# A pooling mixer fed from a transposed copy of the input, with its neighbour sums on VectorE

## The reference, cut to what matters

```python
h = rms_norm(x, g_mix)
for g, win in enumerate((2, 4, 8, 16)):          # 256 channels each
    mean = (cs[t + win//2] - cs[t - win//2]) / cnt    # centred window, cut at the sequence's ends
    d[g] = mean - h[:, slice(g)]
y = einsum('bsgc,gce->bsge', d, pool_w) * pool_scale
x = x + y
a = relu(rms_norm(x, g_mlp) @ w_up)
x = x + (a * a) @ w_down
return rms_norm(x, g_fin)
```

## Time and profile before

| | |
|---|---|
| median of 3 runs | 1790.71 us (1789.93 to 1791.59) |
| the profiled execution | 1790.22 us, its span 1788.4 |
| busy, share of the span | PE 98%, PEld 82%, DVE 63%, ACT 43%, POOL 9% |
| granted TensorE clock, mean | 0.996 |
| DMA | 432.67 MB, 242 GB/s |

### The profile page before, as it was taken

One profiled execution on the slowest core, in us unless ns is written; L12 is line 12 of the kernel. 1 busy time (PEld: TensorE's weight loads), 2 busy tenths in 40 slices (PEclk: granted clock), 3 DMA queues, 4 the chain that ended last, 5 costly groups with the idle time before them and its releaser, 6 DMA issues.

```text
span 1788.4 us, 20968 instructions
## 1 busy us (share of the span) xinstructions
PE 1756.3 (98%) x8156; PEld 1461.8 (82%) x8156; DVE 1122.7 (63%) x1178; ACT 761.4 (43%) x1186; POOL 158.7 (9%) x139
## 2 busy tenths in 40 slices
PE   8999999999999999999999999999999999999996
PEld 8888887778888888888888888888888888888885
DVE  6678888786555564765555647645556575445447
ACT  6556554554343335344333344343333543233232
POOL 4000112001001120010011200000112010000001
PEclk9999999999999999999999999999999999999998
DMA  7597766668856665668666555776665657666654
GB/s 266 218 348 281 265 252 242 245 263 326 307 212 224 223 224 212 247 242 295 243 223 223 213 212 204 280 295 223 224 224 212 235 205 273 240 223 239 233 202 163
DMA packets 80902, 432.67 MB, mean 242 GB/s; under 512 B 8860, under 2 KB 10780, under 8 KB 42916
## 3 DMA queue, kind: packets, MB, share of 16 engines
q1 hardware_dynamic: 57764, 347.44, 52.6%
q10 hardware_dynamic: 23040, 83.90, 13.8%
HBM read 360.00 MB, written 71.30 MB: 241 GB/s over the span
## 4 chain that ended last, share of the span: by engine, by line
PE 89%; DVE 6%; ACT 1%; DMA 1%; issue 1%; POOL 1%; ACTq 0%; SPq 0%; POOLq 0%; DVEq 0%
PE up_ps L1169 16%; PE up_ps L1171 16%; PE up_ps L1170 16%; PE ring_ps L1188 13%; PE ring_ps L1190 13%; PE ring_ps L1189 13%; DVE m_acc L832 1%; PE ring_ps L1213 1%; DVE w_slot L765 1%; PE ring_ps L1215 1%; PE ring_ps L1214 1%; DVE a_slot L773 1%; PE mix_ps L1198 1%; DVE wu_lo L756 1%; DMA wd_raw<-w_down 1%
## 5 line engine op out<-in xcount | busy, mean ns | idle before, releaser
L756 DVE TENSOR_TENSOR wu_lo<-wu_raw,wu_hi 128x1024 fp32r<-128x1024 f32 x158 | 195.8, 1239 | 579.7 <-ACT wu_hi L496 579.7
L1169 PE MATMUL up_ps<-h_hi,wu_hi 128*128 128x512 f32 x1280 | 501.4, 392 | 0.6 <-DVE h_lo L897 0.6
L1171 PE MATMUL up_ps<-h_hi,wu_lo 128*128 128x512 f32 x1280 | 498.5, 389 | 0.0
L1170 PE MATMUL up_ps<-h_lo,wu_hi 128*128 128x512 f32 x1280 | 498.5, 389 | 0.0
L533 ACT ACTIVATE a_raw<-up_ps 128x512 f32<-128x512 f32 x160 | 95.3, 596 | 509.0 <-PE up_ps L1171 509.0
L832 DVE TENSOR_TENSOR m_acc<-ring_ps,m_acc 128x1024 f32<-128x1024 f32 x245 | 298.6, 1219 | 18.8 <-PE ring_ps L1190 18.4
L1188 PE MATMUL ring_ps<-w_slot,a_slot 128*128 128x512 f32 x760 | 296.8, 391 | 1.1 <-DVE m_acc L832 1.1
L1190 PE MATMUL ring_ps<-w_slot,a_slot 128*128 128x512 f32 x760 | 295.9, 389 | 0.0
L1189 PE MATMUL ring_ps<-w_slot,a_slot 128*128 128x512 f32 x760 | 295.7, 389 | 0.0
L1171 PEld LDWEIGHTS up_ps<-h_hi,wu_lo 128*128 128x128 f32 x1280 | 240.2, 188 | 50.5
L1169 PEld LDWEIGHTS up_ps<-h_hi,wu_hi 128*128 128x128 f32 x1280 | 240.3, 188 | 49.4 <-DVE h_lo L897 1.2
(11 more groups left out here) (136 smaller groups left out, 1642.2 us busy)
## 6 DMA issues: line engine op xcount, KB each, us to landing
w_slot<-w_cache SPq DMA_DIRECT2D x134, 1024.0 KB, 5.1
w_more<-w_cache SPq DMA_DIRECT2D x90, 1024.0 KB, 5.1
wu_raw<-w_up ACTq DMA_DIRECT2D x160, 512.0 KB, 3.2
w_cache<-w_slot SPq DMA_DIRECT2D x56, 1024.0 KB, 4.9
wd_raw<-w_down SPq DMA_DIRECT2D x16, 1024.0 KB, 8.7
xr<-x SPq DMA_DIRECT2D x20, 512.0 KB, 7.6
out<-m_acc SPq DMA_DIRECT2D x20, 512.0 KB, 5.6
pw_slot<-pw_cache SPq DMA_DIRECT2D x16, 512.0 KB, 4.3
```

Source lines behind the costliest of these rows:

```text
L756: nc.vector.tensor_tensor(wu_lo[:, u % FT, :, :], wu_raw[:, u % FT, :, :], wu_hi[:, u % FT, :, :].bitcast(f32), ALU.subtract).then_inc(wu_ ...
L1169: nc.tensor.matmul(o, hi, h2_hi[:, d, :], start=(d == 0), stop=False)
L1170: nc.tensor.matmul(o, hi, h2_lo[:, d, :], start=False, stop=False)
L1171: last = nc.tensor.matmul(o, lo, h2_hi[:, d, :], start=False, stop=(d == DT - 1))
```

## The change

The host now also gives `x_turned`: for groups 1 to 4 the input transposed, with halos, in slices of one window (128 partitions x 2 x 528 columns). SyncE loads a slice into one of two buffers `xt`. The scales, which stand one per partition in `rs_x`, are written by ScalarE as a row to HBM (`store_rs`, three DMAs, step 2) and loaded back to all partitions (`load_rs`, step 3); GpSimd multiplies the slice by them (`scale_turned`). The transposes, `norm_rows`, `keep_turned`, `keep_turned_halos`, `xw` and `ht` are gone. The neighbour sums move from GpSimd to VectorE, one level per call: level 0 ahead of the second split of up weights, levels 1 and 2 ahead of the third, level 3 and the end scaling behind the eviction of P4. The own term and the low split now follow P7's eviction; ScalarE's high split moves ahead of the fourth `activate`. On TensorE the pooled product goes behind the fourth up tile, so that P2 follows it. `add_pooled` moves behind `split_wu(4n+5)` and `sum_a(n, P5)`.

```diff
 SyncE
             def load_halos(m):
                 if m > 1:
-                    sp.wait_ge(xw_done, NORMS * WINDOWS * (m - 1))
+                    sp.wait_ge(ms_x_done, NORMS * (m - 1))
+            def load_turned(m, w):
+                v = WINDOWS * (m - 1) + w
+                if v >= 2:
+                    sp.wait_ge(diff_done, v - 1)
+                sp.dma_start(xt[:, w % 2, :, :], x_turned[m - 1, w]).then_inc(xt_in[w % 2], 16)
                     load_ends(g + 1)
+                    load_turned(g + 1, 0)
+                    load_turned(g + 1, 1)
                     load_pool_w(g + 1, 0)
...
                     load_pool_w(g + 1, s - WINDOW_STEP + 1)
+                if mixes and WINDOW_STEP <= s < WINDOW_STEP + WINDOWS - 2:
+                    load_turned(g + 1, s - WINDOW_STEP + 2)
 ScalarE
+            def store_rs(m):
                 act.wait_ge(rs_x_done, m)
+                row = rs_rows[m - 1]
+                act.dma_start(row[HALO:HALO + GT].rearrange("(j p) -> p j", p=P), rs_x[:, 0:TT],
+                              allow_slow_non_contiguous=True).then_inc(rs_stored, 16)
...
+            def load_rs(m):
+                act.wait_ge(rs_stored, 16 * ROW_PARTS * m)
+                if m > 1:
+                    act.wait_ge(xt_scaled, CT * WINDOWS * (m - 1))
+                act.dma_start(rs_b[:, :], rs_rows[m - 1].partition_broadcast(P)).then_inc(rs_b_in, 16)
             def split_pooled(m, w):
                 act.wait_ge(diff_done, WINDOWS * (m - 1) + w + 1)
+                if w > 0:
+                    act.wait_ge(ring_full, TURN[(m, w - 1, 1)] + 1)
...
-                if windows:
-                    keep_turned(g + 1, w)
                 activate(4 * n)
                 split_wu(4 * n + 2)
+                if mixes and s == WINDOW_STEP:
+                    load_rs(g + 1)
...
-                if windows:
-                    split_pooled(g + 1, w)
...
                 split_a(q0 + 7)
+                if windows:
+                    split_pooled(g + 1, w)
                 split_w(q0 + 8)
-                if mixes and 0 <= s - STATS_STEP < WINDOWS:
-                    norm_rows(g + 1, s - STATS_STEP)
+                if mixes and s == STATS_STEP:
+                    store_rs(g + 1)
                 activate(4 * n + 3)
 VectorE
+            def window_sum(m, w, level):
+                if level > w:
+                    return
...
+                if level == 0:
+                    dve.wait_ge(xt_scaled, CT * (WINDOWS * (m - 1) + w + 1))
...
+                else:
+                    dve.wait_ge(summed, before)
+                nc.vector.tensor_tensor(dst[:, :, first + to:first + to + n], src[:, :, first:first + n],
+                                        src[:, :, first + shift:first + shift + n], ALU.add).then_inc(summed, 1)
                     split_w(q0 + P4)
+                if windows:
+                    window_sum(g + 1, w, 0)
                 split_wu(4 * n + 3)
...
                 if windows:
-                    subtract_own(g + 1, w)
-                    split_pooled(g + 1, w)
+                    window_sum(g + 1, w, 1)
+                    window_sum(g + 1, w, 2)
                 split_wu(4 * n + 4)
                 if n > 0:
                     evict(q0 + P4)
                     split_a(q0 + P2)
+                if windows:
+                    window_sum(g + 1, w, 3)
+                    scale_ends(g + 1, w)
+                if n > 0:
                     evict(q0 + P7)
+                if windows:
+                    subtract_own(g + 1, w)
+                    split_pooled(g + 1, w)
                 sum_w(n, P5)
                 split_w(q0 + NP + P1)
                 split_a(q0 + NP + P1)
-                if windows:
-                    add_pooled(g + 1, w)
                 split_w(q0 + NP + P5)
                 sum_w(n, P7)
                 sum_w(n, P6)
                 split_wu(4 * n + 5)
                 sum_a(n, P5)
+                if windows:
+                    add_pooled(g + 1, w)
                 if n > 0:
                     evict(q0 + P2)
 GpSimd
-            def next_sums(m, w):
...
+            def scale_turned(m, w):
+                v = WINDOWS * (m - 1) + w
+                slot = xt[:, w % 2, :, :]
+                pool.wait_ge(xt_in[w % 2], 16 * (v // 2 + 1))
+                pool.wait_ge(rs_b_in, 16 * m)
+                for c in range(CT):
+                    nc.gpsimd.tensor_tensor(slot[:, c, :], slot[:, c, :], rs_b[:, :], ALU.mult).then_inc(xt_scaled, 1)
 TensorE
-                if windows:
-                    turn_window(g + 1, w)
                 up_tile(4 * n)
                 product(q0 + 0)
                 product(q0 + 1)
-                if windows:
-                    turn_halos(g + 1, w)
...
                 product(q0 + 5)
+                up_tile(4 * n + 3)
                 if windows:
                     pool_out(g + 1, w)
-                up_tile(4 * n + 3)
                 product(q0 + 6)
```

More of the change, by code:

```diff
@@ L23 @@
 RING = 4
-TURNS = CT + 1
+ROW_PARTS = 3
 FP = 4
@@ L114, in slot_before, with build @@
     return q - W_SLOTS - W_MORE if q >= CACHED + W_MORE else None
-def build(nc, x, halos, w_up, w_down, pool_w, pool_scale, g_mix, g_mlp, g_fin, ends, bands, ident_in,
-          w_cache, pw_cache, out):
+def build(nc, x, halos, x_turned, w_up, w_down, pool_w, pool_scale, g_mix, g_mlp, g_fin, ends, bands, ident_in,
+          w_cache, pw_cache, rs_rows, out):
     f32 = mybir.dt.float32
@@ L171, in build @@
         xh = sb("xh", [2 * HALO, D])
-        xw = sb("xw", [P, NORMS, WC])
-        ht = sb("ht", [P, CT, HT])
+        xt = sb("xt", [P, 2, CT, HT])
+        rs_b = sb("rs_b", [P, HT])
         end_scale = sb("end_scale", [P, WINDOWS, CT, 2, HALO])
@@ L308, in build @@
         rs_x_done = sem("rs_x_done")
-        xw_done = sem("xw_done")
-        x_turned = sem("x_turned")
-        ht_done = sem("ht_done")
+        rs_stored = sem("rs_stored")
+        rs_b_in = sem("rs_b_in")
+        xt_in = [sem(f"xt_in{i}") for i in range(2)]
+        xt_scaled = sem("xt_scaled")
         summed = sem("summed")
@@ L337, in stores_of_slot @@
             return sum(1 for p in range(min(q, CACHED)) if weight_slot(p) == weight_slot(q))
[L339 to L354, removed]
         @block.sync
@@ L546, in row_stats @@
                     mean_square(src, ms_x[0:rows, j:j + 1], rows).then_inc(ms_x_done, 1)
-            def norm_rows(m, w):
+            def store_rs(m):
                 act.wait_ge(rs_x_done, m)
[L550 to L569, removed]
+                row = rs_rows[m - 1]
@@ new lines, in store_rs @@
+                act.dma_start(row[HALO:HALO + GT].rearrange("(j p) -> p j", p=P), rs_x[:, 0:TT],
+                              allow_slow_non_contiguous=True).then_inc(rs_stored, 16)
+                act.dma_start(row[0:HALO].rearrange("(p j) -> p j", j=1), rs_x[0:HALO, TT:NORMS]).then_inc(rs_stored, 16)
+                act.dma_start(row[HALO + GT:HT].rearrange("(p j) -> p j", j=1),
+                              rs_x[HALO:2 * HALO, TT:NORMS]).then_inc(rs_stored, 16)
+            def load_rs(m):
[3 more added lines that the diff above has]
+                act.dma_start(rs_b[:, :], rs_rows[m - 1].partition_broadcast(P)).then_inc(rs_b_in, 16)
@@ L677, in step @@
                 split_w(q0 + 4)
-                if windows:
-                    keep_turned_halos(g + 1, w)
                 if mixes and s == MIXED_STEP:
@@ L882, in first_add_pooled, with scale_ends @@
                                             ALU.add).then_inc(first_read, 1)
+            def window_sum(m, w, level):
+                if level > w:
+                    return
+                src, dst = xt[:, w % 2, :, :] if level == 0 else sums[(level - 1) % 2], sums[level % 2]
+                before = SUM_STEPS[WINDOWS] * (m - 1) + SUM_STEPS[w] + level
+                shift, first = 2 ** level, HALO - 2 ** w
+                n = GT + 2 ** (w + 1) - 2 * shift
+                to = 2 ** w if level == w else 0
+                if level == 0:
+                    dve.wait_ge(xt_scaled, CT * (WINDOWS * (m - 1) + w + 1))
+                    if WINDOWS * (m - 1) + w > 0:
+                        dve.wait_ge(dt_lo_done, WINDOWS * (m - 1) + w)
+                else:
+                    dve.wait_ge(summed, before)
+                nc.vector.tensor_tensor(dst[:, :, first + to:first + to + n], src[:, :, first:first + n],
+                                        src[:, :, first + shift:first + shift + n], ALU.add).then_inc(summed, 1)
+            def scale_ends(m, w):
+                ends_of = sums[w % 2][:, :, HALO:HALO + GT].rearrange("p c (a b) -> p c a b", b=HALO)
+                both = ends_of[:, :, 0:GT // HALO:GT // HALO - 1, :]
+                dve.wait_ge(ends_in, 16 * m)
+                dve.wait_ge(summed, SUM_STEPS[WINDOWS] * (m - 1) + SUM_STEPS[w + 1] - 1)
```

(9 more changed lines are left out.)

8 lines of the change are left out of this document (3 added, 5 removed).

## The result

The changed kernel takes 1836.45 us (median of five runs, 1835.14 to 1839.79) against 1790.71 on the same chip: a ratio of 1.0257, 95% interval 1.0243 to 1.0271. It is slower, as forecast, but 1815 and the range up to 1832 were too low. The profiled execution took 1836.45 us, 46.2 more than that of before.

A forecast was written before the change was run, and what follows sets the result against it. TensorE, busy 98% of the span, was taken as the bound: 1790.2 - 18.1 (transposes) - 10.3 (pooled waits) + 23.8 and 22.6 (P2's waits) + 6.4 (slow clock) = 1814.6, say 1815 us; range 1804 to 1832.

The forecast's parts named there:

- transposes gone: TensorE's window and halo transposes removed: 1.13 us in each of 16 window steps, 18.1 us saved, nothing hiding them.
- waits before the pooled product gone: TensorE's waits there, with slow matmuls behind the longest, go because VectorE gains an up tile's time: 10.3 us saved.
- P2 behind the addition, groups 1 to 3: P2, ready at T + 3.0, starts at T + 4.98 (T: fourth up tile issued): 1.98 us lost x 12, 23.8 us.
- the same, group 0: P2 waits longer behind down-weight work: 5.4 us in windows 0 to 2, 6.5 in window 3, 22.6 us.
- pooled product waits in windows 3: Level 3 delays dt_lo, so the pooled product waits 0.6 us; in groups 1 to 3 this only shortens P2's wait.
- slow clock behind P2's waits, group 0: All four idles lower the clock; the half-rate stretch behind each loses 1.6 us, 6.4 us in all.
- slow clock behind P2's waits, groups 1 to 3: Costed at nothing, since a 1.9 us idle in the old profile had not lowered the clock.
- window 0 of group 0: No cost beyond its P2 wait and slow clock; stores, transfers and scale loading were taken as covered.
- The mechanism: P2 needs add_pooled of half 0 for its ring turn; VectorE runs that behind operations needing the finished fourth up tile.
- rival 2: The 2 us waits in groups 1 to 3 lower the clock too, 1.6 us each, 19 us: 1834; chance 12%.
- the load of the scales: In each group's first window, issued at S + 8.2 (S: first up tile's start), landing 9.7 us later, 2.4 to spare.
- Rival 1: P2 does not wait for the addition, so the change gives the 28.4 us it takes off: 1762; chance 5%.

The follow-up runs named there:

- e1: The changed kernel with add_pooled moved back behind split_a of the next P1, ahead of split_w(P5) and split_wu(4n+5); 1773.41 us, ratio 0.9906 to the kernel before.
- e3: The kernel before, with only TensorE's order (pooled product behind the fourth up tile) and the place of add_pooled from the change; 1837.46 us, ratio 1.0261.
- e7: The changed kernel with the pooled product back ahead of the fourth up tile on TensorE, VectorE's order unchanged; 2003.4 us, ratio 1.1181.
- e2: The changed kernel with TensorE turning the identity into unused PSUM between pooled product and P2, filling most of the wait; 1821.46 us, ratio 1.0172.
- e5: e1 with the scales stored as 128 pieces of 16 bytes in place of 512 of 4, GpSimd reading with a stride; 1772.66 us, ratio 0.9893.
- e9: e5 with level 3 of the sums directly behind levels 1 and 2, and ScalarE's split_pooled ahead of split_w and split_a; 1765.00 us, ratio 0.9854.
- e4: The changed kernel with the store of the scales issued behind the last up-weight load of its step; 1845.46 us, ratio 1.0309.

## Why the prediction was right in its sign and short in its size

The terms, between the two profiled executions (starts measured as distances above 0.227 or 0.12):

| term | forecast | measured |
|---|---|---|
| transposes gone | -18.1 | -18.2 (what the starts around them lose before) |
| waits before the pooled product gone | -10.3 | -10.7 (6.0 waits, 1.4 slow clock, 3.3 small steps) |
| P2 behind the addition, groups 1 to 3 | +23.8 | +24.2 (9 x 2.17, 3 x 1.53) |
| the same, group 0 | +22.6 | +21.8 (4.6, 5.6, 5.6, 6.1) |
| pooled product waits in windows 3 | within the above | +2.4 (4 x 0.6) |
| slow clock behind P2's waits, group 0 | +6.4 | +8.7 (2.7, 2.3, 2.1, 1.5) |
| slow clock behind P2's waits, groups 1 to 3 | 0 | +9.6 (6 times 1.6) |
| small steps behind P2's waits (0.31 for 0.23 and the like) | 0 | +1.0 |
| window 0 of group 0 | 0 | +5.4 idle, +1.4 slow clock |

1. *The mechanism was right, and so was the size of the waits.* 46.4 us were forecast, with the pooled product's 0.6 in windows 3 in them, and 48.4 came: 46.0 in front of P2 and 2.4 in front of the pooled product. e1 takes them away by one move, e3 makes them on the old kernel, and e7 shows the end of the addition near T + 5 without the pooled product as cover.

2. *The step that failed* is the one that gave the short waits of groups 1 to 3 no slow clock: forecast 0, measured 9.6 us. I had one row for it, an idle of 1.74 us, and took it as a bound for 1.98. The same 2.02 us idle lowered the clock 6 times in 9. Without the slow clock behind all 16 waits, group 0's included, the kernel took 15.0 us less (e2). Group 0's share, 6.4, had been sized at 1.6 a wait from one slow stretch of 3.3 us; three of its four waits cost 2.1 to 2.7. By the Trainium skill (TensorE: Matmul & The Clock Gate, HAM oscillation) idle gaps are what throttles TensorE, every time where they are long enough; the traces agree for 4.28 us and more, and show both outcomes at 2.0. My rival 2 had this mechanism at all 12 waits and 19 us; it came at half of them. Its 1834 lay outside my range, which ended at 1832 and so did not take in this rival, as I had written; without window 0 of group 0, below, the time would have been inside it.

3. *The second failed step* is window 0 of group 0, costed at nothing. I watched the load of the scales; GpSimd could start at 163.9, about 1.5 us later than the estimate had it, and this nearness was luck: the load was issued 6.2 us later than estimated, behind the held ScalarE, and took 4.9 us in place of 9.7. What failed was that I dismissed the store of the scales as three short issues: the issue is short, but the load of up weights behind it took 12.4 us. e5, with larger pieces, has it at 7.9, so about 4.5 us of the 12.4 were the store's. Then ScalarE's dt_hi, which I had only priced by duration, stood behind a split that waits for down weights; e9 shows it. And GpSimd's four products took 7.4 us, 1.86 each where I took 1.4, with VectorE beside them. VectorE, then GpSimd:

```profile
167.75 2.35 DVE L754 TENSOR_TENSOR w_slot<-t_sum,w_slot 128x1024 fp32r<-128x1024 f32 x1
170.03 2.35 DVE L888 TENSOR_TENSOR sums<-xt 128x1024 f32<-128x1024 f32 x1
...
163.87 7.43 POOL L1143 TENSOR_TENSOR xt<-xt,rs_b 128x528 f32<-128x528 f32 x4 [25.88 <-DMA rs_b<-rs_rows]
```

VectorE's operations with two SBUF inputs took 2.35 in place of 1.22, as the rule of the Trainium skill (SBUF — State Buffer, Who interferes with whom) has it. By itself this cost TensorE nothing: in e5 the same two took 2.58 and 2.56 beside GpSimd, and no product waited. The 0.8 us in each group's first window that I had worked out beside the sum did not come in groups 1 to 3 either.

4. Rival 1 (1762) gave what the change is worth without P2's wait. e1, at 1773.4, still holds window 0; e9, without that and the waits of windows 3, has 1765.0. So the 28.4 us taken off were nearly right; the rows measured give 28.9.

The measured rows sum to 45.7 of the 46.2. Which of the 2.0 us waits lower the clock stays open.

## What to carry to other kernels

When a piece of work moves on the bounding engine, look at what now stands directly behind it and which turn of a shared ring that needs; the release may sit behind instructions that wait for the engine's own latest result, and then each move costs a full round trip. Price an idle of the matrix engine with its slow stretch behind it, also a 2 us one, and use one example of no penalty as a chance and not as a bound. A small DMA is not a short one: what its queue carries next pays for its many pieces.

## What the runs showed of the hardware

The granted clock behind an idle of TensorE, over the profiled executions of the changed kernel, e3 and e4: after 1.1 to 1.5 us it never fell (0 of 16), after 1.96 to 2.02 us in the window steps of groups 1 to 3 in 18 of 30, after 4.28 us and more always (10 of 10), with 1.5 to 2.7 us lost each time. (In e2 it fell behind an idle of 1.89 us and not behind one of 1.76.) Identical waits with identical surroundings came out both ways in one execution. ScalarE issued a store of 512 separate 4-byte elements in 0.4 us, and the 512 KB load behind it on the same queue landed 12.4 us after its issue; with the same bytes in 128 pieces of 16 it landed after 7.9.
